# Expert loop with each expert's last product moved between the halves of the next expert's first product, a weight queue in the same order, memory values at every second step, and the first W1 in four column pieces

## The chip, the cores and the metric

The kernel runs on one core of one Trainium2 chip. The metric is the device time of one execution in microseconds (us); the runs of one kernel differ by some tenths of a per cent. TensorE (PE in the profile) multiplies, VectorE (DVE) and ScalarE (ACT) move results out of PSUM and do the element-wise work, GpSimd (POOL) builds selection matrices and issues the indirect transfers, and SyncE (SP) issues the weight transfers.

## What is computed

One layer for 512 prompt tokens and 8 sample tokens, 1024 wide. Three branches (short convolution, stick-breaking attention, attention over a memory of 256 tokens) are gated, summed and multiplied by an output matrix. A mixture of 32 experts follows: each token picks one of four groups and two of its eight experts. Cut to the parts that matter here:

```python
def cross_attend(qx, mk, mv):                       # samples: mk, mv from a cache of 8 requests
    s = jnp.einsum('bthd,bmhd->bhtm', qx, mk) * (X_HEAD_DIM ** -0.5)
    p = jax.nn.softmax(s, axis=-1).astype(mv.dtype)
    return jnp.einsum('bhtm,bmhd->bthd', p, mv)

def run_block(a):                                   # per expert e, on the rows that chose it
    xb, e = a
    return (jax.nn.silu(xb @ w1[e]) * (xb @ w3[e])) @ w2[e]
```

W1 and W3 of an expert are 1024 x 512 and W2 is 512 x 1024, all in float32: 2 MiB each, 6 MiB for an expert, and every expert is run.

## The kernel before, in words

Each engine has its own hand-written program; semaphores order them. Nothing is scheduled by a tool, so the order of the code is the order on each engine and in each queue.

**Front part.** The input projection runs as chunks of 128 columns, each a product in three passes (high times high, high times low, low times high parts; `three_pass`, line 800). In the middle of the kernel eight turns compute a gate chunk (`three_pass`) and a branch chunk (`branch`, line 946) of the convolution branch. Between these products stand sixteen small steps, `point(0)` to `point(15)`, `point(2n)` behind the gate chunk of turn n and `point(2n+1)` behind its branch chunk. The steps carry the attention over the prompt's memory and the sample rows' scores and values. The value products of the eight sample rows are `two_values(0, b, pm_t)` for b = 0, 2, 4, 6, two rows at a time; before, they stand in steps 11, 12, 13 and 14. Their data are the tiles `vals`, two slots of 512 KB. ScalarE issues the transfers (`load_memory_values(b)`, line 1659), and each pair of rows waits for `val_used`, that is until the pair before it has been multiplied. VectorE then adds the halves of the result (`two_out`), and `turn_four` turns them.

**Between the parts.** The output product (`merge_out(i)`, line 1192) runs tile by tile for four prompt tiles, with the router between. It reads `m_hi`, which lies where W1 of expert 0 goes later, so SP waits until all four tiles are done (`wo_ps` at 2 * NT) and then loads W1 of expert 0 in two transfers of 1 MiB. Then come the last 128 rows of `h` into DRAM, W2 of expert 1, W3 and W2 of expert 2.

**Expert loop.** Expert n has slot n % 3 for its weights. PE does for expert n: `up_and_gate` (lines 1379 and 1380: W1 and W3 side by side on the two halves of the array, 16 pairs of matmuls, 8 for each half of the 1024 input rows), `give(n-1, (0, 1))` (line 1401: two of the four tiles of expert n-1's result go back to the tokens by a selection matrix `spread`), `turn_up` and `turn_rows` (transposes, line 767), `give(n-1, (2,))`, `down` (lines 1426 and 1427: W2, 8 pairs), `give(n-1, (3,))`. VectorE copies the up result (`up_out`, line 2556), forms the activation (`act_out`, lines 2563 and 2565), moves the next gathered rows (`rows_out`, line 2545), adds the returned tiles to `x1` (`added`, line 2573) and forms `y_rest` (line 2568) from the down product once ScalarE has written `y_top` (line 1869). Before `y_top`, ScalarE copies the sample rows (line 1865). SP loads for expert e, into the slot of expert e-3: the two halves of W1 and W3 as each half has been used (`up_ps`), then W2 (`y2_ps`). Rows of `h` are gathered by POOL for two experts at a time, 128 rows of 4 KB.

## Time and profile before

| what | value |
|---|---|
| median of 3 runs | 1066.97 us (1065.58 to 1070.71) |
| the profiled execution, its own time | 1069.17 us |
| its span | 1067.3 us |
| PE busy | 1033.1 us, 97% of the span |
| DVE, ACT, POOL busy | 55%, 31%, 14% |
| moved by DMA | 278.42 MB, mean 261 GB/s |
| granted TensorE clock, mean | 0.991 |

Busy is the time in which an engine has an instruction in work. PE's share is high everywhere, so it alone doesn't say whether PE is at its limit: a matmul that waits for weights at its start counts only from its start. The rows of forty slices show PE's share and what the DMA engines moved side by side.

### The profile page before, as it was taken

To read this page: it belongs to the slowest core of one execution; us is meant where nothing else is said; L and a number is where in the kernel's file an instruction comes from. 1 tells how busy PE (TensorE), PEld (TensorE's weight loads), DVE (VectorE), ACT (ScalarE), POOL (GpSimd) and SP (SyncE) were. 2 spreads that over 40 slices of the span, in tenths; PEclk is the share of its full clock that TensorE was granted. 3 is DMA by queue.
4 is the path that set the end of the run, shared out by engine and by line. 5 is a ranking of instruction groups with operands and counts; after the bars stand their busy time and mean duration, and the time that the engine had idled before them with its cause. 6 is when DMAs were issued, how large, how long until landed. Compare 5 with 4: busy or idle time off the path is not lost.

```text
span 1067.3 us, 16248 instructions
## 1 busy us (share of the span) xinstructions
PE 1033.1 (97%) x6634; PEld 696.6 (65%) x6634; DVE 586.4 (55%) x940; ACT 325.6 (31%) x471; POOL 147.2 (14%) x180
## 2 busy tenths in 40 slices
PE   9999999999989999999999999999999999999996
PEld 8999998988868788999776433443334334334432
DVE  5222265877767866543546655555555555455545
ACT  6322233155546544322445011111111111111111
POOL 0000000002313564000000311101111101111100
PEclk9999999999999999999999999999999999999999
DMA  5723131545462232552445999999999999999982
GB/s 203 261 94 98 62 100 60 191 137 182 151 221 75 83 123 87 211 201 83 164 182 220 424 427 424 426 426 427 426 425 425 429 424 426 426 426 429 424 350 80
DMA packets 51274, 278.42 MB, mean 261 GB/s; under 512 B 7542, under 2 KB 7814, under 8 KB 30728
## 3 DMA queue, kind: packets, MB, share of 16 engines
q1 hardware_dynamic: 42360, 254.26, 59.3%
q0 software_dynamic: 6048, 16.86, 4.8%
q10 hardware_dynamic: 2800, 6.36, 1.7%
q8 instruction: 48, 0.79, 0.3%
q14 instruction: 18, 0.15, 0.0%
HBM read 274.09 MB, written 7.48 MB: 264 GB/s over the span
## 4 chain that ended last, share of the span: by engine, by line
PE 86%; DVE 4%; DMA 3%; ACT 2%; POOL 2%; issue 2%; ACTq 0%; SPq 0%; POOLq 0%; DVEq 0%
PE acc_all L800 25%; PE acc_all L1379 20%; PE acc_all L1426 10%; PE acc_all L1401 7%; PE acc_all L767 6%; PE acc_all L946 5%; PE acc_all L1192 3%; POOL beta L435 1%; DMA vals<-in_cache_mem_v 1%; DMA xg<-h_dram,pair_row 1%; PE acc_all L1063 1%; PE acc_all L1427 1%; POOL keep L435 1%; PE acc_all L876 1%; PE acc_all L875 1%
## 5 line engine op out<-in xcount | busy, mean ns | idle before, releaser
L800 PE MATMUL acc_all<-xn_hi,w_hi 128*128 128x260 f32 x832 | 172.3, 289 | 8.7 <-DVE gate_sb L2131 4.3
L800 PE MATMUL acc_all<-xn_hi,w_lo 128*128 128x260 f32 x832 | 168.6, 284 | 0.0
L800 PE MATMUL acc_all<-xn_lo,w_hi 128*128 128x260 f32 x832 | 168.2, 284 | 0.0
L2573 DVE TENSOR_TENSOR x<-x,acc_all 128x1024 f32<-128x1024 f32 x127 | 151.4, 1213 | 1.1 <-PE acc_all L1401 1.1
L800 PEld LDWEIGHTS acc_all<-xn_hi,w_hi 128*128 128x128 f32 x832 | 129.7, 190 | 16.2 <-DVE gate_sb L2131 6.6
L800 PEld LDWEIGHTS acc_all<-xn_lo,w_hi 128*128 128x128 f32 x832 | 129.4, 190 | 0.0
L800 PEld LDWEIGHTS acc_all<-xn_hi,w_lo 128*128 128x128 f32 x832 | 129.2, 190 | 0.0
L724 POOL TENSOR_SCALAR spread<-tok_row,slots 128x512 fp32r<-128x512 f32 x32 | 50.2, 1568 | 370.2 <-PE acc_all L1401 370.2
L1958 DVE TENSOR_TENSOR w_lo<-w_raw,w_hi 128x1024 fp32r<-128x1024 f32 x52 | 63.4, 1222 | 67.7 <-ACT w_hi L1564 67.5
L1865 ACT ACTIVATE few<-acc_all,slots 8x512 f32<-8x512 f32 x64 | 43.4, 679 | 153.5 <-PE acc_all L1427 121.0
L1859 ACT ACTIVATE gate_h<-acc_all 128x256 f32<-128x256 f32 x32 | 12.3, 384 | 234.6 <-PE acc_all L767 234.6
L2556 DVE COPY up_sb<-acc_all 128x512 f32<-128x512 f32 x32 | 22.1, 691 | 104.9 <-PE acc_all L1380 104.9
L1379 PE MATMUL acc_all<-w_a,xg_t 128*64 128x512 f32 x176 | 78.1, 595 | 0.6 <-DVE xg_t L2462 0.6
L1379 PE MATMUL acc_all<-w_b,xg_t 128*64 128x512 f32 x176 | 78.1, 595 | 0.4 <-DVE xg_t L2545 0.4
L1380 PE MATMUL acc_all<-w_b,xg_t 128*64 128x512 f32 x176 | 78.1, 595 | 0.0
L1380 PE MATMUL acc_all<-w_a,xg_t 128*64 128x512 f32 x176 | 78.1, 595 | 0.0
L1379 PE MATMUL acc_all<-w_c,xg_t 128*64 128x512 f32 x160 | 70.8, 595 | 0.1
L1380 PE MATMUL acc_all<-w_c,xg_t 128*64 128x512 f32 x160 | 70.8, 595 | 0.0
L2568 DVE SCALAR_TENSOR_TENSOR y_rest<-acc_all,slots,y_top 128x512 fp32r<-128x512 f32 x32 | 24.0, 750 | 84.8 <-ACT y_top L1869 84.8
L1401 PEld LDWEIGHTS acc_all<-y_top,spread 64*128 64x128 f32 x256 | 23.9, 183 | 58.3 <-issue 32.6
L1401 PE MATMUL acc_all<-y_top,spread 64*128 64x512 f32 x256 | 60.7, 469 | 0.7 <-DVE x L2573 0.7
L1564 ACT ACTIVATE w_hi<-w_raw 128x1024 fp32r<-128x1024 f32 x52 | 54.5, 1051 | 7.4 <-DMA w_raw<-in_w_in 7.4
(389 smaller groups left out, 1855.2 us busy)
## 6 DMA issues: line engine op xcount, KB each, us to landing
w_a<-in_w SPq DMA_DIRECT2D x44, 1024.0 KB, 17.2
w_b<-in_w SPq DMA_DIRECT2D x44, 1024.0 KB, 18.0
w_c<-in_w SPq DMA_DIRECT2D x40, 1024.0 KB, 17.7
w_raw<-in_w_in SPq DMA_DIRECT2D x52, 512.0 KB, 3.7
w_a<-in_w SPq DMA_DIRECT2D x11, 2048.0 KB, 18.3
w_b<-in_w SPq DMA_DIRECT2D x11, 2048.0 KB, 18.6
w_c<-in_w SPq DMA_DIRECT2D x10, 2048.0 KB, 18.7
w_br<-in_w_branch SPq DMA_DIRECT2D x24, 256.0 KB, 4.5
```

Source lines behind the costliest of these rows:

```text
L724: pool.tensor_scalar(spread[n % 2][:, :], tok_row[:, :], slot_tok[:, n:n + 1], None, ALU.is_equal).then_inc(spread_ok, 1)
L767: return pe.transpose(out, in_, ident[0:k, 0:k])
L800: mm = pe.matmul(out[:, a, :], w[:, slot, k, :], x[:, k, a * HALF_TOK:(a + 1) * HALF_TOK], start=first, stop=last)
L946: mm = pe.matmul(out[:, a, :], w, x[:, a * HALF_TOK:(a + 1) * HALF_TOK], start=begin, stop=end)
L1379: pe.matmul(bank(5)[0:CAP, :], lhs, w1_sb[w][:, k, :], start=(k == 0), stop=(k == KD - 1))
L1380: mm = pe.matmul(bank(5)[CAP:P, :], lhs, w3_sb[w][:, k, :], start=(k == 0), stop=(k == KD - 1))
L1401: mm = pe.matmul(bank(out + half), spread[hot][at, tok(t)], y[at, :], start=first and alone, stop=not first, skip_group_check=not alone)
L1426: pe.matmul(bank(7)[0:CAP, :], act_t[:, c, :], w2_sb[w][:, c, 0:DE], start=(c == 0), stop=(c == CW - 1))
L1564: act.activation(w_hi[:, slot, :, :], w_raw[:, slot, :, :], ACT.Copy).then_inc(split_hi, 1)
L1865: act.activation(few[n // QUADS % 2][half][strip:strip + NB, :], bank(7)[at, :], ACT.Copy, scale=slot_gate[at, n:n + 1]).then_inc(few_in, 1)
L1958: dve.tensor_tensor(w_lo[:, slot, :, :], w_raw[:, slot, :, :], w_hi[:, slot, :, :].bitcast(F32), ALU.subtract).then_inc(split_lo, 1)
L2573: dve.tensor_tensor(x1[:, t, :], x1[:, t, :], bank(2 * pair, 2), ALU.add).then_inc(back_ok, 1)
```

## The change

Four edits.

1. **Expert loop on PE.** The product is cut in its halves (`up_part`), and the down product of expert n-1 now stands between the two halves of expert n's up product, with tiles 2 and 3 of expert n-2's result ahead of it. Tiles 0 and 1 of expert n-1 follow the second half. DVE's order follows: two adds come right behind `up_out`, two behind `rows_out`, and `y_rest` of expert n comes last in the turn, now waiting for a down product that PE reaches in the next turn.
2. **Weight queue.** SP loads in the order of use: first half of W1 and W3 of expert e, W2 of expert e-1, second half of W1 and W3 of expert e. Both halves of expert 3 are issued ahead of the loop.
3. **W1 of expert 0** comes in four pieces of 128 columns, each issued when one tile of the output product is done. A piece is 512 KB in runs of 512 bytes.
4. **Memory values.** `two_values(0, b)` stands in steps 11, 13 and 15, and the fourth behind the gate product after the eight turns; `two_out` and `load_memory_values(6)` move with them, and `cross_values(XH - 1)` goes ahead of the two `turn_four`.

```diff
-            sp.wait_ge(wo_ps, 2 * NT)
-            load_up(0, 0, w1_sb, w1_d)
+            for t in range(NT - 1):
+                sp.wait_ge(wo_ps, NT + 2 + t)
+                sp.dma_start(w1_sb[0][:, :, tok(t)], w1_d[0][:, :, tok(t)]).then_inc(w13_ld[0][0], 16)
...
-            def load_expert(e, j, before):
-                load_up(e, j, before=before)
-
+            def load_down(e, j, before):
                 sp.wait_ge(y2_ps, before)
                 sp.dma_start(w2_sb[j][:, :, :], w2_d[e]).then_inc(w2_ld[j], 16)
 
+            def load_turn(e, j, before):
+
+                load_up(e, j, before=before, parts=(0,))
+                load_down(e - 1, (j - 1) % WS, before - 1)
+                load_up(e, j, before=before, parts=(1,))
+
+            load_up(WS, 0, before=1)
             with sp.Fori(0, NE // WS - 1) as i:
-                for j in range(WS):
-                    load_expert(WS * i + WS + j, j, WS * i + j + 1)
...
-                if 11 <= p < 15:
+                if p in (11, 13, 15):
                     pe.wait_ge(pmt_sb, 1)
-                    two_values(0, 2 * (p - 11), pm_t)
+                    two_values(0, p - 11, pm_t)
...
             turn_probs(2 * XH - 1)
+            two_values(0, 6, pm_t)
+            cross_values(XH - 1)
             pe.wait_ge(yg_sb, 4)
             turn_four(0, 0, 5)
             pe.wait_ge(cs_exp, 4 * XH)
             turn_four(0, 1, 6)
-            cross_values(XH - 1)
...
+            for n in range(1, NE):
                 p, j = divmod(n, 2)
-                if n >= 1:
-                    pe.wait_ge(xgt_sb, 2 * p + 2)
-                    pe.wait_ge(up_ok, n)
-                up_and_gate(n % WS, p % 2, j, n // WS + 1, n)
-                if n >= 1:
-                    give(n - 1, (0, 1))
+                w, loads = n % WS, n // WS + 1
+                pe.wait_ge(xgt_sb, 2 * p + 1)
+                pe.wait_ge(up_ok, n)
+                up_part(w, p % 2, j, loads, 0)
...
+                    give(n - 2, (2, 3))
+                    pe.wait_ge(rest_ok, n - 1)
+                    down((n - 1) % WS, (n - 1) // WS + 1, n - 1)
+                pe.wait_ge(xgt_sb, 2 * p + 2)
+                up_part(w, p % 2, j, loads, 1)
+                give(n - 1, (0, 1))
                 pe.wait_ge(up_ok, n + 1)
                 turn_up()
...
+            give(NE - 2, (2,))
+            pe.wait_ge(rest_ok, NE - 1)
+            down((NE - 1) % WS, (NE - 1) // WS + 1, NE - 1)
...
-                if n in (5, 6):
-                    two_out(0, 4 * (n - 5))
+                if n >= 5:
+                    two_out(0, 2 * (n - 5))
```

How the instructions move. In the rows below, `w_a`, `w_b`, `w_c` are the three weight slots, "waits" names the semaphores, and "..." stands for the rest of a run of matmuls.

PE, one turn in the middle of the expert loop (up product in slot a), before:

```order
L1379 MATMUL acc_all<-w_a,xg_t 64x512 [waits w13_ld0a,up_ok,xgt_sb]
...
L1379 MATMUL acc_all<-w_a,xg_t 64x512 [waits w13_ld0b]
...
L1401 MATMUL acc_all<-y_top,spread_180 128x512 [waits rest_ok,spread_ok,back_ok]
...
L767 MATMUL acc_all<-ident,up_sb 128x128 [waits up_ok]
...
L767 MATMUL acc_all<-ident,xg_173 128x128 [waits xgt_sb,xg_ld1]
...
L1401 MATMUL acc_all<-y_top,spread_180 128x512 [waits back_ok]
...
L1426 MATMUL acc_all<-w_a,act_t 64x512 [waits actt_ok,w2_ld0,rest_ok]
...
L1401 MATMUL acc_all<-y_top,spread_180 128x512 [waits back_ok]
...
```

The same turn in the changed kernel:

```order
L1385 MATMUL acc_all<-w_a,xg_t 64x512 [waits w13_ld0a,up_ok,xgt_sb]
...
L1400 MATMUL acc_all<-y_top,spread_179 128x512 [waits back_ok]
...
L1425 MATMUL acc_all<-w_c,act_t 64x512 [waits actt_ok,w2_ld2,rest_ok]
...
L1385 MATMUL acc_all<-w_a,xg_t 64x512 [waits w13_ld0b,xgt_sb]
...
L1400 MATMUL acc_all<-y_top,spread_180 128x512 [waits rest_ok,spread_ok,back_ok]
...
L775 MATMUL acc_all<-ident,up_sb 128x128 [waits up_ok]
...
L775 MATMUL acc_all<-ident,xg_172 128x128 [waits xgt_sb,xg_ld0]
...
```

The down product (slot c, the expert before) now stands between the two halves of the up product; the transposes `up_sb` are no longer followed by the product that needs their activation.

DVE, the same turn, from the activation to the copy of the next up result, before:

```order
L2565 TENSOR_TENSOR act_t<-gate_h,acc_all 128x128 [waits half_ok]
L2545 TENSOR_TENSOR xg_t<-acc_all,norm_pk 128x512 [waits xgt_ps]
L2573 TENSOR_TENSOR x_103<-x_103,acc_all 128x1024 [waits back_ps] x2
L2568 SCALAR_TENSOR_TENSOR y_rest<-acc_all,slots,y_top 128x512 [waits top_ok]
L2573 TENSOR_TENSOR x_103<-x_103,acc_all 128x1024 [waits back_ps]
L2556 COPY up_sb<-acc_all 128x512 [waits upt_ps,up_ps]
L2573 TENSOR_TENSOR x_103<-x_103,acc_all 128x1024 [waits back_ps]
```

and in the changed kernel:

```order
L2576 TENSOR_TENSOR act_t<-gate_h,acc_all 128x128 [waits half_ok]
L2556 TENSOR_TENSOR xg_t<-acc_all,norm_pk 128x512 [waits xgt_ps]
L2584 TENSOR_TENSOR x_103<-x_103,acc_all 128x1024 [waits back_ps] x2
L2579 SCALAR_TENSOR_TENSOR y_rest<-acc_all,slots,y_top 128x512 [waits top_ok]
L2567 COPY up_sb<-acc_all 128x512 [waits upt_ps,up_ps]
L2584 TENSOR_TENSOR x_103<-x_103,acc_all 128x1024 [waits back_ps] x2
```

The adds (`x_103` is `x1`) now come in two pairs, and nothing stands between `y_rest` and the copy of the up result.

## Rows read from the trace of the kernel before

**Rows 1.** The page: PE's busy time, and DMA share in 40 slices.

```profile
PE 1033.1 (97%) x6634; PEld 696.6 (65%) x6634; DVE 586.4 (55%) x940; ACT 325.6 (31%) x471; POOL 147.2 (14%) x180
...
DMA  5723131545462232552445999999999999999982
```

**Rows 2.** Stretches of the span: busy time by engine, PEclk, DMA share, GB/s.

```profile
core 0: us, PE busy (x) PEld busy (x) DVE busy (x) ACT busy (x) POOL busy (x), PEclk, DMA share, GB/s
300.00:304.50 4.50, 3.27 (x15) 1.64 (x16) 3.98 (x6) 1.20 (x4) 1.89 (x2) 0.62 0.24 62
555.00:565.00 10.00, 10.00 (x59) 8.71 (x59) 5.80 (x26) 6.01 (x7) 0.00 (x0) 1.00 0.14 54
740.00:840.00 100.00, 99.23 (x508) 39.51 (x506) 51.98 (x76) 17.00 (x28) 15.25 (x11) 1.00 1.01 427
```

**Rows 3.** DVE's copies of the up result, one an expert, all 32.

```profile
L2556 DVE COPY up_sb<-acc_all x32: 690/692/694, 594.7 to 1046.6; 128x512 f32<-128x512 f32 x32
```

**Rows 4.** Timeline from expert 30 to 31: start, duration, engine, instruction [idle before].

```profile
1032.12 0.50 PE L1401 MATMUL acc_all<-y_top,spread 64*128 64x512 f32 x2
1035.22 0.61 PE L1426 MATMUL acc_all<-w_a,act_t 128*64 128x512 f32 x1 [0.31 <-DVE act_t L2565]
1038.91 1.38 ACT L1865 ACTIVATE few<-acc_all,slots 8x512 f32<-8x512 f32 x2 [4.48 <-PE acc_all L1427]
1039.47 0.64 PE L1379 MATMUL acc_all<-w_b,xg_t 128*64 128x512 f32 x1
1041.04 0.75 DVE L2568 SCALAR_TENSOR_TENSOR y_rest<-acc_all,slots,y_top 128x512 fp32r<-128x512 f32 x1 [3.19 <-ACT y_top L1869]
1042.95 0.59 PE L1379 MATMUL acc_all<-w_b,xg_t 128*64 128x512 f32 x1
1046.49 0.50 PE L1401 MATMUL acc_all<-y_top,spread 64*128 64x512 f32 x2
1049.58 0.61 PE L1426 MATMUL acc_all<-w_b,act_t 128*64 128x512 f32 x1 [0.31 <-DVE act_t L2565]
```

**Rows 5.** SP's queue: the last loads of expert 31, second half and W2.

```profile
1004.40 3.01 SPq L546 DMA_DIRECT2D w_b<-in_w  x1
1010.18 0.33 SPq L580 DMA_DIRECT2D w_b<-in_w  x1
```

**Rows 6.** Time to landing: W3 half at 1004.40, W2 at 1010.18, W2 at 603.25.

```profile
DMA to landing us min/median/max: 30.4/30.4/30.4
DMA to landing us min/median/max: 29.5/29.5/29.5
DMA to landing us min/median/max: 12.3/12.3/12.3
```

**Rows 7.** SP's queue ahead of the expert loop.

```profile
572.08 1.06 SPq L546 DMA_DIRECT2D w_a<-in_w  x2
577.65 0.33 SPq L569 DMA_DIRECT2D h_dram<-h_tok  x1
578.02 0.43 SPq L570 DMA_DIRECT2D w_b<-in_w  x1
584.24 1.39 SPq L546 DMA_DIRECT2D w_c<-in_w  x2
```

**Rows 8.** Chain of waits, steps 11 to 13.

```profile
292.09 9.00 DMA vals<-in_cache_mem_v
```

**Rows 9.** PE's timeline, steps 12 to 15.

```profile
301.23 1.94 PE L997 MATMUL acc_all<-vals,pm_t 128*32 128x512 f32 x8 [1.77 <-DMA vals<-in_cache_mem_v]
303.10 0.80 PE L946 MATMUL acc_all<-y_hi_conv,w_br_hi_conv 128*128 128x260 f32 x2
306.72 0.49 PE L956 MATMUL acc_all<-q_parts,both_r 40*128 40x512 f32 x1
310.07 1.06 PE L997 MATMUL acc_all<-vals,pm_t 128*32 128x512 f32 x8 [0.95 <-DMA vals<-in_cache_mem_v]
319.95 0.51 PE L946 MATMUL acc_all<-y_hi_conv,w_br_hi_conv 128*128 128x260 f32 x2
323.01 0.50 PE L956 MATMUL acc_all<-q_parts,both_r 40*128 40x512 f32 x1
```

**Rows 10.** A gate chunk in the chain, and DMA issues of 512 KB: time to landing.

```profile
492.71 5.74 PE acc_all L800 x48
...
w_raw<-in_w_in SPq DMA_DIRECT2D x52, 512.0 KB, 3.7
vals<-in_cache_mem_v ACTq DMA_DIRECT2D x8, 512.0 KB, 5.1
```

More of the change, by code:

```diff
@@ L536, in _, with load_up @@
                 load_branch(n + RING)
-            def load_up(e, j, *which, before=None):
-                for part in range(2):
+            def load_up(e, j, *which, before=None, parts=range(2)):
+                for part in parts:
                     if before is not None:
@@ L1369, in turn_rows, with up_part @@
                 turn_pair(p % 2, half)
[L1371 to L1388 removed]
+            def up_part(w, slot, j, loads, part):
+                pe.wait_ge(w13_ld[w][part], 32 * loads + (FIRST_LOADS[part] if w == 0 else 0))
+                for k in range(part * KD // 2, (part + 1) * KD // 2):
+                    lhs = xg_t[:, slot, k, CAP * j:CAP * (j + 1)]
+                    pe.matmul(bank(5)[0:CAP, :], lhs, w1_sb[w][:, k, :], start=(k == 0), stop=(k == KD - 1))
+                    mm = pe.matmul(bank(5)[CAP:P, :], lhs, w3_sb[w][:, k, :], start=(k == 0), stop=(k == KD - 1))
+                mm.then_inc(up_ps, 1)
             def turn_up():
@@ L1690, in _ @@
                     load_memory_values(max(0, 2 * (n - 4)))
-                if n == 6:
-                    load_memory_values(6)
                 if n % 2 == 0 and n >= 2:
@@ L2597, in _ @@
                 if n >= 1:
-                    added(n - 1, (0,))
+                    added(n - 1, (0, 1))
                 else:
                     over_first()
+                if n == 1:
+                    rows_out(1, 0)
                 dve.wait_ge(sig_ok, n + 1)
@@ L2617, in _ @@
                 elif n == 1:
-                    rows_out(1, 0)
+                    rows_out(1, 1)
                 elif n + 2 < NE:
@@ L2621, in _ @@
                 if n >= 1:
-                    added(n - 1, (1, 2) if n < NE - 1 else (1, 2, 3))
-                if n == 1:
-                    rows_out(1, 1)
-                dve.wait_ge(top_ok, n + 1)
-                y_rest_out(slot_gate[:, n:n + 1])
-                if 1 <= n < NE - 1:
-                    added(n - 1, (3,))
+                    added(n - 1, (2, 3))
+                if n >= BATCH and n % BATCH == 0:
+                    add_few(n // BATCH - 1)
                 if n == 1:
```

72 lines of the change are left out of this document (32 added, 40 removed).

## Prediction

> **What bounds the kernel now.** Four views, in this order. The page first: PE is busy 97% of the span, and from the 23rd slice on DMA is full as well [rows 1]; two resources may bind in the second half. The stretches tell what "full" is: 427 GB/s at a share of 1.01 [rows 2]. An expert needs 6.29 MB of weights and half of a gather (0.26 MB), 6.55 MB, so the transfers take 15.3 us an expert. PE takes less: from the give of expert 30's turn at 1032.12 to that of expert 31 at 1046.49 is 14.37 us [rows 4], and over all 31 steps (1046.6 - 594.7) / 31 = 14.6 us with the start and the long turns [rows 3]. So PE sets the pace and eats a store of loads that were issued early. The queue's view shows it: a W2 load took 12.3 us to land at the start of the loop and the last ones took 30 us [rows 6], though each is issued as soon as its slot is free. The last view is how much store is left at the end: the second half of W3 of expert 31 lands at 1004.40 + 30.4 = 1034.8, W2 at 1010.18 + 29.5 = 1039.7 [rows 5, 6]; PE needs them at 1042.95 and 1049.58 [rows 4]. That is 8.15 and 9.9 us. **A faster PE can win those 8.15 us and no more, unless the stream itself ends earlier.** Ahead of the loop PE is alone, so what it saves there moves PE and the stream together.
>
> **Memory values.** Step 12 waits 1.77 us for its transfer (9.00 us long) and step 13 waits 0.95 us [rows 8, 9]. Behind the first wait the granted clock in 300 to 304.5 is 0.62 of full speed [rows 2], between the levels of 1.2 and 2.4 GHz: step 12's values take 1.87 us to the next product instead of about 1.0, and the branch chunk 306.72 - 303.10 = 3.62 instead of 323.01 - 319.95 = 3.06 [rows 9]. Together 1.77 + 0.87 + 0.56 + 0.95 = 4.2 us. In the new order a gate chunk (5.74 us, [rows 10]), a branch chunk (3.06) and the small products lie between two value steps, over 10 us, against 9.00 us for the longest load: no wait. The fourth pair has only the gate chunk and a transpose ahead of it, about 6.3 us, against 5.1 us at the median [rows 10] and 9.00 at the worst: between no wait and 3 us. ScalarE's `load_memory_values(6)` also holds its next split back until step 15, which the gate chunk covers. I take -4.2, bounds -4.4 and -1.
>
> **First W1.** In 555 to 565 the queues move 54 GB/s [rows 2]; three of the four pieces (1.57 MB) now go there, at no cost to anybody. But the stream isn't shortened by all of 1.57 / 0.427 = 3.7 us: SP issues the fourth piece at 572.08, then must wait for `h` at 577.65 and for the router at 584.24 [rows 7], so the queue now runs dry at two places. By 584.24 SP had issued 4.7 MB before (W1, `h`, W2); 12.2 us at 427 would carry 5.2 MB, less some 2 us of start (an estimate), 4.3. So 0.4 MB stood over, and up to 1.1 if the stream was slower in its start; now next to nothing to 0.6. The stream behind it gains 1 to 2 us; I take 1.6. What no row shows is a hardware-queue load in runs of 512 bytes. From below, a piece costs its bytes, 1.2 us. From above, each run costs as much as a 4 KB one, eight times the bytes, 9.8 us: then the last piece takes 4.9 us more than the whole W1 did, and the stream loses 4.9 instead of gaining 1.6. I take the bytes, since `w_raw`, of the same 512 KB, lands in 3.7 us [rows 10], start included, and the last piece isn't needed for 14 us. The Trainium skill, "DMA: Bandwidth & Descriptors", section "Measured (HBM→SBUF, 128 partitions, SWDGE, issued from GpSimd)", speaks against cutting: it asks for 1 MiB or more a transfer, gives 341 GB/s there and 138 GB/s at 64 KB. By it, an estimate, a piece takes 1.5 to 3.8 us instead of 1.2, and my gain of 1.6 would be -1.0 to 1.3. No run here shows it yet.
>
> **Expert loop, PE.** Work is the same: 16 and 8 pairs, four tiles given back, eight transposes. What goes is the wait of the down product for the activation, 0.31 us [rows 4], since half an up product and two tiles now stand between; and of six changes between kinds of product one goes (up, give, turn, give, down, give before; up, give, down, up, give, turn now). A change shows as the rest between 8 pairs at 0.43 us (3.44) and the 3.54 us from 1042.95 to 1046.49 [rows 4]: 0.1. I take 0.41 us a turn, bounds 0.15 (a part given back by the cut in the up product) and 0.6. For experts 3 to 31 that is 29 x 0.41 = 11.9 us. In the turns of experts 1 and 2 two things cancel: the wait for both halves of the turned rows goes, but two adds now stand ahead of `rows_out`; I take +0.6 for them, bounds -1 and +2.
>
> A wait is added: tiles 0 and 1 of expert n-1 need `y_rest`, whose down product now ends only half an up product earlier. Its chain, from ACT's start at 1038.91 to DVE's end at 1041.04 + 0.75 = 1041.79, is 2.9 us, 3.1 with the start [rows 4]; the cover is the half, 3.5 us. It is hidden with 0.4 us to spare. Behind `y_rest` on DVE stands the copy of the up result, which needs the same half to end, so it isn't held up.
>
> **Weight queue.** The new order is PE's new order. With the stream's end at 1039.7 - 4.2 - 1.6 = 1033.9, and 4.9 us for 2.1 MB, W2 of expert 31 lands at 1033.9, the second half of W1 and W3 at 1029.0, W2 of expert 30 at 1024.1, the first half at 1019.2. A PE that nobody holds reaches the second half at 1042.95 - 4.2 + 0.6 - 11.9 = 1027.5, so it waits 1.5 us there. In the old order the first half would land 4.9 us later, when PE has long asked for it: this edit gives nothing by itself and is what lets the first be used.
>
> **Sum.** PE alone: -4.2 + 0.6 - 11.9 = -15.5 us. The stream: -4.2 - 1.6 - 8.15 = -13.95. The smaller holds, and both ends lie so close that I take -13.9. The profiled execution, 1069.17 us, is 2.2 us above the median; against it 1055.3, against the median 1066.97 **1053.1 us**, -1.3%. A measurement of this kernel tells 0.5%, 5.3 us, from no change.
>
> **Rivals.**
> - *The turn gains little* (0.15 us: the cut costs what the wait gave). PE: -4.2 + 0.6 - 4.4 = -8.0, 1059.0. For it: PE's rests between kinds of product are modelled, not measured. Chance 0.15.
> - *A front edit fails*: pieces at the upper bound, -13.95 + 6.5 = -7.4, 1059.5; or a full wait for the fourth pair, -11, 1056. Chance 0.13.
> - *The clock falls in the loop.* At the end PE waits for weights in each turn. After 1.77 us of waiting the clock was halved at 301, which cost 1.4 us; the wait of 0.95 us at 309 brought nothing [rows 2, 9]. One to three such drops: -12.5 to -9.7, 1054.5 to 1057.3. Chance 0.10. The Trainium skill, "TensorE: Matmul & The Clock Gate", section "HAM oscillation — how this bites in real kernels", has this as a pattern of loops that wait for loads; by the rows above it needs longer waits than I forecast.
> - *The loop closes over `y_rest`* (slower). The give waits whenever ACT's copy of the sample rows, `y_top` and `y_rest` take more than 3.5 us. Each us over is paid 29 times. It eats all of -15.5 when the chain is 4.03 us, and at 4.4 us the kernel is at 1066.97 - 15.5 + 26 = 1077.5. Against it: the rows give 3.1 us, and no new work on either engine. Chance 0.04.
> - *The interleaving does nothing* because some other wait holds each turn at 14.37: only the front gain, 1062.8. Chance 0.05.
> - *The stream ends earlier than I think* (all 3.7 us of the pieces): 1051.5, or 1050. Chance 0.05.
>
> **The numbers.** The forecast has 0.48, with 1051.5 to 1055.5 as its own range. The range 1049.5 to 1060.5 leaves out the slower case, the no-gain case and the edges of the others. Faster by over 0.5% are all but the last part of the front failures, the `y_rest` case and the no-gain case: 0.89; within 0.5%: 0.07; slower 0.04.
>
> **What would show it.** No wait for `vals` in steps 11 to 15, and no low clock near 300. The last W2 lands about 5.8 us earlier than at 1039.7. Turns of about 13.95 us in the middle of the loop, near 15.3 at the very end with PE waiting for weights, and the down product without the 0.31 us for `act_t`. Wrong would be: a wait of the give for `y_rest` in every turn; turns of 14.3; DMA that isn't full between 600 and 1030.

## The result, and the profile after

The changed kernel takes 1059.03 us (median of 6 runs, 1057.1 to 1063.23) against 1067.88 us for the kernel before on the same chip: a ratio of 0.9938, 95% interval 0.9917 to 0.9959. Timed again later beside its variants it came to 1058.72 us and a ratio of 0.9908 (0.9889 to 0.9928). So the change gives 0.6 to 0.9%, 7 to 10 us, where 1.3% was forecast. One of the twelve executions of experiment 1 below took 3538.6 us; it counts as slow and is left out of the ratio. The profiled execution has a span of 1060.5 us and took 1062.32 us; forecast for it was 1055.3 us, 7.0 less.

The page of the changed kernel: PE's busy time, the DMA share in 40 slices, and the chain that ended last.

```profile
PE 1024.3 (97%) x6634; PEld 692.2 (65%) x6634; DVE 586.5 (55%) x940; ACT 325.6 (31%) x471; POOL 147.0 (14%) x180
...
DMA  5632232545453242452454999999999999999993
...
PE 76%; DMA 9%; SPq 5%; DVE 4%; ACT 2%; POOL 2%; issue 2%; ACTq 0%; POOLq 0%; DVEq 0%
```

The chain now holds 9% of DMA and 5% of SP's queue, against 3% and 0% before: the weights are on it. DVE's copies of the up result, one an expert, cut the run into three parts:

```profile
L2567 DVE COPY up_sb<-acc_all x32: 690/692/694, 594.6 to 1039.5; 128x512 f32<-128x512 f32 x32
```

Against [rows 3]: up to the first copy 594.7 became 594.6, where -4.2 was forecast; from the first copy to the last 451.9 became 444.9, -7.0 where -9.75 (8.15 of store and 1.6 of a shorter stream) was; from the last copy to the end 20.7 became 21.0. What is missing is 4.1 + 2.7 + 0.3 = 7.1 us. So two terms failed, one ahead of the loop, one in the stream. The two executions are alike ahead of the loop: both have four low clocks there, three at the same places (near 120, 219 and 577 us) and one in the memory values (near 301 before, 328 now).

**The turn takes the forecast time.** Two copies in a row, and the new cover of `y_rest` (start, duration, engine, instruction, idle time before):

```profile
641.10 0.69 DVE L2567 COPY up_sb<-acc_all 128x512 f32<-128x512 f32 x1 [0.56 <-PE acc_all L1386]
655.07 0.69 DVE L2567 COPY up_sb<-acc_all 128x512 f32<-128x512 f32 x1 [0.56 <-PE acc_all L1386]
...
665.62 1.38 ACT L1877 ACTIVATE few<-acc_all,slots 8x512 f32<-8x512 f32 x2 [8.36 <-PE acc_all L1426]
667.02 0.69 ACT L1881 ACTIVATE y_top<-acc_all,slots 128x512 fp32r<-128x512 f32 x1
667.74 0.75 DVE L2579 SCALAR_TENSOR_TENSOR y_rest<-acc_all,slots,y_top 128x512 fp32r<-128x512 f32 x1 [3.83 <-ACT y_top L1881]
668.93 0.50 PE L1400 MATMUL acc_all<-y_top,spread 64*128 64x512 f32 x2
```

A turn takes 13.97 to 13.99 us, against 14.36 before; every eighth, which has the sample rows' product as well, takes 14.95 (15.34 before). `y_rest` is done at 668.49 and the give starts at 668.93: 0.44 us to spare.

The time isn't made up as forecast, though. The 0.31 us wait of the down product in [rows 4] stands only in the last two turns, which have no `turn_rows`. In the middle of the loop the kernel before looks like this:

```profile
788.34 0.50 PE L1401 MATMUL acc_all<-y_top,spread 64*128 64x512 f32 x2
...
788.75 0.29 DVE L2565 TENSOR_TENSOR act_t<-gate_h,acc_all 128x128 f32<-128x128 f32 x1
...
789.18 0.61 PE L1426 MATMUL acc_all<-w_b,act_t 128*64 128x512 f32 x1
```

No wait is shown before the down product. It does start 0.14 us behind the end of its activation (789.04; 0.15 us in the last turns), and 0.84 us behind the start of the tile ahead of it, where the same kind of product ahead of an up product takes 0.66: 0.18 us that can be called waiting. One turn of each kernel by its parts, each from its first product to the next part's, in us:

| | up | tiles given back | transposes | down | turn |
|---|---|---|---|---|---|
| before (786.09 to 800.45) | 7.02 | 1.14 + 0.84 + 0.66 | 1.11 | 3.59 | 14.36 |
| change (643.22 to 657.20) | 3.58 + 3.54 | 1.13 + 1.14 | 1.11 | 3.48 | 13.98 |

So 0.18 us are the wait for the activation, 0.19 come from giving tiles 2 and 3 back together (1.32 became 1.13), 0.11 from a shorter down product (why isn't shown), and the cut in the up product takes 0.10 back.

**The memory values** still have a wait. PE's timeline, and the chain around it:

```profile
326.59 1.07 PE L1005 MATMUL acc_all<-vals,pm_t 128*32 128x512 f32 x8 [1.86 <-DMA vals<-in_cache_mem_v]
327.59 3.59 PE L993 MATMUL acc_all<-prob_t,mv 128*128 128x512 f32 x4
...
332.07 2.43 PE L1071 MATMUL acc_all<-proj 64*128 64x256 f32 x16
```

```profile
316.94 1.49 ACT y_hi_x L1730
318.43 0.33 ACTq L1672
...
318.79 7.66 DMA vals<-in_cache_mem_v
```

Both waits of [rows 9] are gone. The fourth pair waits 1.86 us, and behind that wait the clock goes down, as it did behind step 12's in [rows 2]:

```profile
core 0: us, PE busy (x) PEld busy (x) DVE busy (x) ACT busy (x) POOL busy (x), PEclk, DMA share, GB/s
300.00:304.50 4.50, 4.50 (x28) 3.45 (x27) 4.43 (x6) 1.62 (x5) 1.89 (x2) 1.00 0.14 32
326.00:331.00 5.00, 4.41 (x13) 1.44 (x14) 1.38 (x2) 0.00 (x0) 0.00 (x0) 0.68 0.00 0
555.00:565.00 10.00, 10.00 (x60) 8.67 (x60) 5.80 (x26) 6.00 (x7) 0.00 (x0) 1.00 0.47 150
575.00:580.00 5.00, 4.94 (x20) 2.17 (x22) 4.22 (x19) 3.54 (x4) 0.00 (x0) 0.70 0.47 145
606.00:608.00 2.00, 2.00 (x46) 1.58 (x46) 0.39 (x3) 0.36 (x1) 1.24 (x2) 1.00 0.83 279
740.00:840.00 100.00, 100.00 (x522) 39.85 (x521) 56.27 (x81) 16.98 (x28) 15.21 (x11) 1.00 1.01 426
```

The first two rows are that low clock: gone from 300, back at 327. The other four are the stream. 555 to 565 now moves 150 GB/s (54 before), but 575 to 580 has a share of 0.47, and 606 to 608 one of 0.83. (PEclk of 0.70 in 575 to 580 is a low clock that the kernel before has at the same place.) The same two stretches before:

```profile
575.00:580.00 5.00, 4.87 (x20) 2.08 (x22) 4.21 (x19) 3.61 (x4) 0.00 (x0) 0.74 0.99 409
606.00:608.00 2.00, 2.00 (x29) 0.88 (x26) 0.00 (x0) 0.00 (x0) 1.78 (x3) 1.00 1.01 430
```

SP's queue in the changed kernel, with the issues around both:

```profile
544.34 28.20 SPq L569 DMA_DIRECT2D w_a<-in_w  x4
577.58 0.34 SPq L571 DMA_DIRECT2D h_dram<-h_tok  x1
...
584.12 1.32 SPq L547 DMA_DIRECT2D w_c<-in_w  x2
...
589.60 5.92 SPq L547 DMA_DIRECT2D w_a<-in_w  x4
606.30 0.82 SPq L547 DMA_DIRECT2D w_b<-in_w  x2
607.38 0.33 SPq L580 DMA_DIRECT2D w_a<-in_w  x1
```

Between 572.5 and 577.58 SP waits for `h`; between 595.5 and 606.30 it waits for a buffer, and the first half of expert 4 and W2 of expert 3 come only then (W2 of expert 3 at 603.25 before, [rows 6]). At the end of the loop the stream is late. SP's last loads, the time to landing of the two halves at 1001.70 to 1006 and of the last W2, and PE's waits:

```profile
1001.70 4.29 SPq L547 DMA_DIRECT2D w_b<-in_w  x2
1006.03 2.41 SPq L580 DMA_DIRECT2D w_b<-in_w  x1
```

```profile
DMA to landing us min/median/max: 29.0/30.4/31.8
DMA to landing us min/median/max: 34.4/34.4/34.4
```

```profile
1020.73 0.61 PE L1385 MATMUL acc_all<-w_a,xg_t 128*64 128x512 f32 x1 [0.43 <-DMA w_a<-in_w]
1035.78 0.62 PE L1385 MATMUL acc_all<-w_b,xg_t 128*64 128x512 f32 x1 [1.29 <-DMA w_b<-in_w]
```

W3's second half lands at about 1003.87 + 31.8 = 1035.7 and PE takes it at 1035.78; before, it landed at 1034.8 and was used at 1042.95. The last W2 lands at 1040.4 (1039.7 before, 1033.9 forecast). The last four turns take 14.46, 15.88, 14.62 and 15.05 us. **The stream ends as late as before, and now PE waits for it.** Between 1000 and 1030 the DMA share is 1.00 to 1.02, so it is the bytes that are late.

### The profile page after: what moved, and what is told of

Same layout as the page of the kernel before. It is cut to its first block, busy times and chain, and to the rows that moved or that the text cites. A ratio compares the mean times of both kernels' runs of the same rounds, so it can differ in the third digit from the quotient of the medians.

```text
span 1060.5 us, 16298 instructions
## 1 busy us (share of the span) xinstructions
PE 1024.3 (97%) x6634; PEld 692.2 (65%) x6634; DVE 586.5 (55%) x940; ACT 325.6 (31%) x471; POOL 147.0 (14%) x180
## 4 chain that ended last, share of the span: by engine, by line
PE 76%; DMA 9%; SPq 5%; DVE 4%; ACT 2%; POOL 2%; issue 2%; ACTq 0%; POOLq 0%; DVEq 0%
PE acc_all L808 26%; PE acc_all L1385 15%; PE acc_all L1425 8%; DMA w_b<-in_w 6%; PE acc_all L954 6%; PE acc_all L1400 5%; PE acc_all L775 5%; SPq L547 4%; PE acc_all L1201 3%; DMA xg<-h_dram,pair_row 1%; POOL beta L436 1%; PE acc_all L1071 1%; SPq L580 1%; PE acc_all L993 1%; PE acc_all L974 1%
## 5 line engine op out<-in xcount | busy, mean ns | idle before, releaser
L1385 PE MATMUL acc_all<-w_b,xg_t 128*64 128x512 f32 x176 | 79.7, 596 | 1.6 <-DMA w_b<-in_w 1.6
L1385 PE MATMUL acc_all<-w_a,xg_t 128*64 128x512 f32 x176 | 79.7, 596 | 1.0 <-DVE xg_t L2473 0.6
L1386 PE MATMUL acc_all<-w_b,xg_t 128*64 128x512 f32 x176 | 79.8, 596 | 0.0
L1386 PE MATMUL acc_all<-w_a,xg_t 128*64 128x512 f32 x176 | 79.8, 596 | 0.0
L1385 PE MATMUL acc_all<-w_c,xg_t 128*64 128x512 f32 x160 | 72.5, 595 | 2.6 <-DVE xg_t L2556 1.5
L1386 PE MATMUL acc_all<-w_c,xg_t 128*64 128x512 f32 x160 | 72.5, 596 | 0.0
L1400 PE MATMUL acc_all<-y_top,spread 64*128 64x512 f32 x256 | 57.5, 444 | 0.6 <-DVE x L2584 0.6
L1585 ACT ACTIVATE proj<-acc_all 128x520 f32<-128x520 f32 (+1 forms) x28 | 16.9, 604 | 124.8 <-PE acc_all L808 118.8
L1385 PEld LDWEIGHTS acc_all<-w_b,xg_t 128*64 128x64 f32 x176 | 23.0, 137 | 47.4 <-issue 47.2
```

The source lines that it names most:

```text
L1385: pe.matmul(bank(5)[0:CAP, :], lhs, w1_sb[w][:, k, :], start=(k == 0), stop=(k == KD - 1))
L1386: mm = pe.matmul(bank(5)[CAP:P, :], lhs, w3_sb[w][:, k, :], start=(k == 0), stop=(k == KD - 1))
L1400: mm = pe.matmul(bank(out + half), spread[hot][at, tok(t)], y[at, :], start=first and alone, stop=not first, skip_group_check=not alone)
```

## The experiments

Two yardsticks stand in each profile, and they are steadier than the absolute times, since low clocks in the front part come and go between executions (the first copy of an up result lay between 587.7 and 596.7 us). *Stretch V* runs from the values of step 11 to the first scores. *Loop L* runs from the first copy of an up result to the last. L has a spread of its own: five profiles whose loop and weight queue are those of the change (the change twice, experiments 2, 6 and 14) lie between 444.5 and 445.6 us. Turns of 13.98 us below always mean those that aren't every eighth.

**1. The values alone**: before, with the value steps of the change.

```diff
-                if 11 <= p < 15:
-                    two_values(0, 2 * (p - 11), pm_t)
+                if p in (11, 13, 15):
+                    two_values(0, p - 11, pm_t)
...
+            two_values(0, 6, pm_t)
+            cross_values(XH - 1)
             pe.wait_ge(yg_sb, 4)
...
-            cross_values(XH - 1)
```

`load_memory_values(6)` and `two_out` move with them as in the change.

> The kernel before with only the value steps moved (the fourth edit). Theory A (the fourth pair's transfer is now the wait): PE waits about 1.9 us for vals behind the gate product, the clock may drop there, and the first score product starts 0 to 1 us earlier than at 332.6; the whole is 0 to 1 us faster than before. Rival (my forecast's term): no wait, -4.2 us, 1063.7. A third outcome, the wait moves but the clock doesn't fall in most runs: about -2 us.

1065.91 us, ratio 0.9993 (0.9979 to 1.0006): nothing that the times can tell. The fourth pair waits 1.76 us; V is 39.31 us. Theory A holds, the forecast's term doesn't.

**2. All but the values**: the change, with the edit of experiment 1 undone.

> The changed kernel with the value steps as before; the other three edits stay. Theory A and the theory that the stream of weights sets the end: the same as the changed kernel within 1 us, since both begin the stream at nearly the same time (1059 to 1060). If the value steps did carry something in ordinary runs, this one is up to 2 us slower than the changed kernel.

1062.09 us, ratio 0.9956 (0.9942 to 0.997). Two waits, 1.51 and 1.33 us, a low clock at 301.4, V 42.35. With the clock the same on both sides the edit shows its worth in V:

| | old value steps | new value steps |
|---|---|---|
| low clock in V | 42.08 (before), 42.35, 42.97 (experiment 8) | 41.12 (change), 41.07 |
| none | 40.41 (experiment 3) | 39.2 to 39.5 (ten profiles) |

1.0 to 1.9 us, not 4.2. By the times this run is 3.1 to 3.4 us above the change (1059.03 and 1058.72), more than the expectation's 2 us and more than V shows, while experiment 1 was only 0.8 us below the kernel before. The clock is what differs: the mean granted clock is 0.993 in these twelve executions, 0.994 in those of the change and 0.9955 in those of experiment 6. With 1060 us times the share of clock that was withheld taken off each execution, an estimate, the edit is worth 1.6 us in experiment 1 (against the kernel before) and 1.5 us here (against experiment 6, timed beside it), which is what V says.

The low clock lies in V in three of the four profiles with the old steps and in two of the twelve with the new. Whether the new steps make it rarer isn't settled by so few; over whole executions experiment 1's mean clock (0.993) is no higher than that of the kernel before (0.994).

**3. The loop alone**: before, with PE's interleaved order, and the old queue, W1 and values.

```diff
-            for n in range(NE):
+            up_part(0, 0, 0, 1, 0)
...
+            for n in range(1, NE):
```

> The kernel before with only the interleaved expert loop: the queue in the old order, W1 of expert 0 in two transfers, value steps as before. Stream theory: turns of 13.98 us until the store of loads is used up, then PE waits for first halves that stand in the queue behind W2s and second halves; the end is 3 to 6 us before that of the kernel before, 1062 to 1065. Rival (the order of the queue doesn't matter, since it is full and bytes decide): within 1 us of the changed kernel, 1059 to 1060.

1065.03 us, ratio 0.998 (0.9966 to 0.9995). Turns of 13.98 us to the copy of expert 22, then 14.38, 15.41, 15.62 (an eighth turn), 14.41, 14.71, 17.6: PE waits for the half that the old order issues late, and behind one wait the clock is down in the loop. L is 448.6 us. The stream theory holds, the rival falls. PE's timeline and the stretch behind it:

```profile
983.75 1.09 PE L1377 MATMUL acc_all<-w_b,xg_t 128*64 128x512 f32 x1 [1.90 <-DMA w_b<-in_w]
```

```profile
983.50:987.50 4.00, 3.75 (x10) 1.27 (x12) 0.80 (x2) 0.00 (x0) 0.00 (x0) 0.57 1.02 432
```

**4. The old queue order**: the change, with `load_expert` as before.

```diff
-                load_up(e, j, before=before, parts=(0,))
-                load_down(e - 1, (j - 1) % WS, before - 1)
-                load_up(e, j, before=before, parts=(1,))
+                load_up(e, j, before=before)
+                sp.wait_ge(y2_ps, before)
+                sp.dma_start(w2_sb[j][:, :, :], w2_d[e]).then_inc(w2_ld[j], 16)
```

> The changed kernel with SP's loop in the old order (both halves of W1 and W3 of an expert, then its W2). Stream theory: no dry spot at 606 to 608, so the stream ends some 0.5 us earlier, but the first half of expert 31 and W2 of expert 30 change places: PE waits for the second half when it has it all; the end within 1.5 us of the changed kernel, rather slower. Rival (the order is what makes the loop work, as I wrote in the prediction): 3 to 5 us slower.

1064.36 us, ratio 0.9965 (0.9947 to 0.9982), L 448.9. The same late turns and the same low clock (984.7). The order is worth 3 to 6 us to the changed kernel; without it L gains 3.0 us instead of 7.0, the low clock's price included. Here the rival holds, and my theory (within 1.5 us) falls.

**5. W1 whole**: the change, with W1 of expert 0 in two transfers of 1 MiB.

```diff
-            for t in range(NT - 1):
-                sp.wait_ge(wo_ps, NT + 2 + t)
-                sp.dma_start(w1_sb[0][:, :, tok(t)], w1_d[0][:, :, tok(t)]).then_inc(w13_ld[0][0], 16)
+            sp.wait_ge(wo_ps, 2 * NT)
+            load_up(0, 0, w1_sb, w1_d)
```

> The changed kernel with W1 of expert 0 in two transfers of 1 MiB at 572. Stream theory: at 192 MB to go the stream is about 0.5 us later than in the changed kernel, but the dry spot at 606 to 608 shrinks, so the end is the same within 1 us. Rival (my forecast's term): 1.6 us slower or more.

1058.81 us, ratio 0.9927 (0.9899 to 0.9954), L 444.8 against 444.9: the pieces give nothing here.

**6. The last values issued early**, on ScalarE.

```diff
+            load_memory_values(6)
             act.wait_ge(br_ps, KD)
             act.wait_ge(cy_sb, XH - 1)
             act.activation(y_hi_x[:, 0:XH - 1, 0:SEQ], proj[:, B0:B0 + XH - 1, 0:SEQ], ACT.Copy).then_inc(xt_hi, 1)
-            load_memory_values(6)
```

> The changed kernel, but ScalarE issues the last memory values before its 1.49 us copy of y_hi_x instead of behind it. Theory A: the transfer starts about 1.1 us earlier, PE's wait falls from 1.86 to 0.5 to 0.9 us, and the clock doesn't fall there; the scores start 2.5 to 3.5 us earlier and the whole is as much faster than the changed kernel (1056). Rival: the transfer is slow because it meets the weight chunk's load, so it lands when it did; no gain.

1058.26 us, ratio 0.9915 (0.9897 to 0.9934). The wait stays, 1.99 us, and V is 39.54. The load goes out as soon as step 15's values have freed the buffer, and takes its 7.8 us. In the changed kernel ScalarE's copy (316.94 to 318.43) lay beside those same values (done at 318.29), so it held the load up by 0.14 us at most. Theory A falls; there is no gain, as the rival says, but for another reason than the rival's. The chain of this version:

```profile
313.71 1.04 PE acc_all L1005 x8
...
314.78 0.37 ACTq L1672
...
315.18 7.79 DMA vals<-in_cache_mem_v
```

**7. Half of W2, changed kernel.**

```diff
-                sp.dma_start(w2_sb[j][:, :, :], w2_d[e]).then_inc(w2_ld[j], 16)
+                sp.dma_start(w2_sb[j][:, 0:CW // 2, :], w2_d[e][:, 0:CW // 2, :]).then_inc(w2_ld[j], 16)
```

> The changed kernel, but from expert 3 on W2's load brings only half of W2 (the first two of four row groups of each partition), so the stream is 17% lighter; the products still run on the whole tile and their results are not the reference's. Stream theory: PE never waits for weights, turns of 13.98 us to the end, the end 4.1 us earlier than in the changed kernel's profile, that is 1055 in the median. Rival (PE waits for something else at the end): the end stays.

1056.18 us, ratio 0.9885 (0.9849 to 0.9922). No wait for weights at all, turns of 13.98 us to the end (the last is 13.54), L 440.2: the stream theory holds. This is PE alone: 451.9 - 440.2 = 11.7 us saved, where the forecast had 11.9 - 0.6 = 11.3. The stream withholds 4.7 of them.

**8. Half of W2, kernel before**, by the same edit.

> The kernel before, whose W2 loads bring only half of each matrix from expert 3 on (so that the stream is 1.05 MB an expert shorter; the output leaves out computing with the right half of W2). My theory: the kernel before is set by PE in the whole loop, its weights were 8 us early at the end, so a lighter stream gives nothing: ratio 0.997 to 1.003, turns of 14.36 us as before, last periods 14.36. Rival (the stream held the kernel before as well, by contention of its transfers with the gathers or by something the waits don't show): 3 to 5 us faster, as with the same cut in the changed kernel, which gave 0.4% against the changed kernel.

1068.61 us, ratio 1.0008 (0.999 to 1.0027), L 451.7. Before, the stream set nothing; the theory holds. The copies of the two, this one and experiment 7:

```profile
L2556 DVE COPY up_sb<-acc_all x32: 691/692/694, 595.4 to 1047.1; 128x512 f32<-128x512 f32 x32
```

```profile
L2567 DVE COPY up_sb<-acc_all x32: 691/692/694, 592.9 to 1033.1; 128x512 f32<-128x512 f32 x32
```

**9. The stream started early**: the change, with W2 of expert 1 right behind W1's last piece, W2 of expert 2 right behind `h` (ahead of the wait for the router), and W2 of expert 3 as soon as expert 0 has used its buffer.

```diff
+            sp.dma_start(w2_sb[1][:, :, :], w2_d[1]).then_inc(w2_ld[1], 16)
             sp.wait_ge(h_ok, NT)
             sp.dma_start(h_dram[tok(MERGE_TILES[NT - 1]), :], h_tok[:, MERGE_TILES[NT - 1], :]).then_inc(h_st, 16)
-            sp.dma_start(w2_sb[1][:, :, :], w2_d[1]).then_inc(w2_ld[1], 16)
+            sp.dma_start(w2_sb[2][:, :, :], w2_d[2]).then_inc(w2_ld[2], 16)
...
-            sp.dma_start(w2_sb[2][:, :, :], w2_d[2]).then_inc(w2_ld[2], 16)
...
             load_up(WS, 0, before=1)
+            load_down(WS, 0, 1)
```

The first three turns of SP's loop are written out, so that the W2 of expert 3 isn't loaded twice.

> The changed kernel with the stream filled in at its start: W2 of experts 1 and 2 are issued right behind the last piece of W1 (W2 of expert 2 behind the rows of h), and W2 of expert 3 as soon as expert 0's is used. Stream theory: the stream ends 4 to 6 us earlier, PE hardly waits any more, the end is 3.5 to 4.5 us earlier than the changed kernel's, 1055. Rival (the waits at the end come from SP's full queue or from the order, not from bytes): no gain. Another rival: the last rows of h land later behind W2 and the first gather with them, which costs 1 to 3 us at the start.

1057.05 us, ratio 0.9892 (0.9854 to 0.993), L 442.3: 2.6 us of the 4.7. The stream theory has the direction, but forecast more: the stream ends 2.6 us earlier, not 4 to 6, and the last two turns are still long (14.56 and 15.09).

**10. Only W2 of expert 3 early**: the last line of 9's diff alone, with the first turns written out as there.

> The changed kernel with one load moved: W2 of expert 3 is issued as soon as expert 0 has used its buffer, not behind the first half of expert 4, where the new order of the queue puts it. My theory: the dry spot at 606 to 608 us goes (DMA share there from 0.83 to 1.0), the stream ends about 1 us earlier measured from the start of the loop, and since the stream sets the end the kernel is 0.5 to 1.2 us faster than the changed one: ratio 0.9925 to 0.993 against before. Rival 1 (what the queue lost there it makes good later, or the gain of the run with both loads moved came from the two loads ahead of the loop): no change against the changed kernel, 0.9938. Rival 2: that run's 2 us all came from this load: 0.991 to 0.992.

1058.21 us, ratio 0.9922 (0.9896 to 0.9948), L 445.2. The dry spot is gone (share 1.03 in 606 to 608), the loop isn't shorter: the first rival.

**11. Only W2 of experts 1 and 2 ahead**: 9's diff without its last line.

> The changed kernel with W2 of experts 1 and 2 issued right behind the last piece of W1 and behind h, ahead of the wait for the router, and W2 of expert 3 where the change has it. My theory: the column pieces moved 1.6 MB into an idle stretch, but the queue then ran dry at the wait for h (share 0.47 in 575 to 580 us, before 0.99), so that nothing came of it; with W2 behind them the stream ends 1.5 to 2.6 us earlier measured from the first copy of an up result (445.5 us in the changed kernel, 442.9 with both moves, 445.9 with the move of W2 of expert 3 alone): 443 to 444, and the last copy 442.3 to 443.4 us behind the first. Rival (both moves are needed): 444.5 or more.

1059.2 us, ratio 0.9921 (0.9901 to 0.9941), L 444.4. My theory wanted 442.3 to 443.4; the rival, that both moves are needed, has it (it said 444.5 or more). The stretches show why:

```profile
596.00:598.00 2.00, 2.00 (x12) 0.76 (x10) 1.82 (x7) 0.00 (x0) 0.00 (x0) 1.00 1.04 438
598.00:600.00 2.00, 2.00 (x12) 0.60 (x10) 1.84 (x5) 0.00 (x0) 0.00 (x0) 1.00 0.66 279
600.00:602.00 2.00, 2.00 (x18) 0.62 (x14) 0.00 (x0) 0.00 (x0) 1.92 (x4) 1.00 0.00 0
602.00:604.00 2.00, 2.00 (x46) 1.39 (x44) 0.52 (x3) 0.60 (x1) 1.07 (x1) 1.00 0.49 78
```

The stream came 4 us early to the point at which SP waits for the next free buffer, and stood still there for as long.

**12. W1 whole, and W2 ahead**: the diffs of 5 and 9.

> The changed kernel with W1 of expert 0 whole, as two transfers of 1 MiB behind the last of its space, W2 of experts 1 and 2 right behind it (ahead of the waits for h and for the router), and W2 of expert 3 as soon as its buffer is free. My theory: the column pieces are worth nothing once the queue has W2 to go on with, since it is full behind W1 in either case, or the later start of W1 costs up to 1.5 us because the pieces used an idle stretch: ratio 0.989 to 0.9915, against 0.9892 with the pieces. Rival (pieces of 512-byte runs cost queue time that the whole transfers don't): faster than with the pieces by 1 us or more, 0.988 or less.

1058.18 us, ratio 0.9919 (0.9893 to 0.9945), L 444.1. My theory is not borne out as it stood: without the pieces L is 1.8 us longer than with them (442.3; 442.7 and 441.5 in experiments 15 and 16), while the times don't part the two. The pieces are worth something once the queue has W2 to go on with, about the 1.6 us that the prediction gave them; only one profile stands on the side without pieces.

**13. The changed kernel again**, as a level for the last set.

> The changed kernel itself, unchanged, beside the variants of this set. It is the level against which they are read: so far variants that should have gained little (0.9922, 0.9919, 0.9915, 0.9927) all came out below the changed kernel's own 0.9938. If that figure was a high sample, it comes out at 0.991 to 0.993 here; if the variants gain, it stays at 0.9935 to 0.994. In the profile: a wait of 1.7 to 2.0 us for the values of the fourth pair, turns of 13.98 us, and 444.5 to 445.5 us from the first copy of an up result to the last.

1058.72 us, ratio 0.9908, L 445.6, V 39.24: its two ratios, 0.9938 and 0.9908, have overlapping intervals, so that 0.9938 needn't be the better figure, and none of experiments 5, 6, 10, 11 and 12 differs from the change by its time. Their verdicts rest on the stretches of their profiles. Nor do the intervals of 9 and 15 part them from the change; there L does (442.3 and 442.7, outside 444.5 to 445.6).

**14. Cross values first**, on PE.

```diff
-            two_values(0, 6, pm_t)
             cross_values(XH - 1)
+            two_values(0, 6, pm_t)
```

> The changed kernel with the product of the last head's cross values put ahead of the fourth pair's values, so that 2 us of PE work lie over the wait. My theory: the memory values' edit brought 1.0 us and not 4.2 because the wait for the fourth pair (1.76 to 1.99 us) took the place of the two waits removed, so hiding part of it shortens the stretch from the values of step 11 to the first scores from 39.35 us (all profiles without a low clock in it) to 38.0 to 38.6 us, with a wait of 0 to 0.7 us for ScalarE's copy in its place; the whole kernel by up to 1 us, which the times can't tell. Rival (the wait isn't on the path: PE would only wait at the scores or the next gate chunk, as it waits 0.86 us for VectorE behind them now): the stretch gets shorter, but a later wait grows by the same, and the next gate chunk starts 14.2 us after the fourth pair's landing as before.

1060.68 us, ratio 0.9932 (0.9913 to 0.9951). The wait for the values is gone, and V is **longer**, 40.12 us. PE's timeline, and two pieces of the chain:

```profile
325.61 1.98 PE L993 MATMUL acc_all<-prob_t,mv 128*128 128x512 f32 x4 [0.74 <-ACT prob_t L1662]
327.53 1.07 PE L1005 MATMUL acc_all<-vals,pm_t 128*32 128x512 f32 x8
330.19 1.09 PE L775 MATMUL acc_all<-ident,y_four 128*128 128x128 f32 x8 [1.60 <-DVE y_four L2173]
331.22 2.43 PE L1071 MATMUL acc_all<-proj 64*128 64x256 f32 x16
```

```profile
324.47 0.60 ACT gate_sb L1652
325.07 0.50 ACT prob_t L1662
```

My theory falls here, and the rival too, since V isn't shorter at all: behind the fourth pair stand VectorE's two steps that make `y_four` (0.69 and 0.70 us), and the cross values had covered them. Moved away, they leave a wait of 1.60 us, and ScalarE's copy one of 0.74. In the change this place is held by a chain: step 15 ends, transfer of 7.7 us, values, `y_four`, turn. In this order another takes over, which has no transfer in it: gate product, ScalarE's two copies, cross values, values, `y_four`, turn. The order of the change is the better one by V (0.8 us); the times don't tell.

**15 and 16. Both repairs**, 6 and 9 together; then with 14 as well.

> The changed kernel with both repairs: ScalarE issues the last memory values ahead of its copy, and the queue has W2 of experts 1 and 2 right behind the last piece of W1 and W2 of expert 3 as soon as its buffer is free. My theory: the two are in different stretches and add, 0.2% of the first (0.9915 against 0.9938) and 0.46% of the second (0.9892): ratio 0.986 to 0.989, 1053 to 1057 us, waits for weights only in the last two or three experts. Rival (the first was only a run without the low clock in the front part, so it gives nothing): 0.989 to 0.990, like the second alone, with the wait for the fourth pair's values at 1.5 to 2 us either way.

1055.56 us, ratio 0.9901 (0.9875 to 0.9928), L 442.7; turns longer than 13.98 us only at the end (14.33 and 15.71). The wait for the fourth pair stays at 1.82 us, V at 39.38: the two don't add, only the stream's repair shows, as the rival says.

> All repairs together: ScalarE issues the last memory values ahead of its copy, the last cross values ahead of them on PE, W2 of experts 1 and 2 right behind W1's last piece and W2 of expert 3 as soon as its buffer is free. My theory: they add, 0.5 to 1.1 us below the version without the change on PE (0.9901, 1055.56 us): ratio 0.988 to 0.990. Rival (front gains come and go with the low clock, and only the stream counts): 0.990 to 0.991.

1056.94 us, ratio 0.9897 (0.9875 to 0.9919), L 441.5, V 40.12. The version of 15 is the fastest by its median, 11 us below the kernel before and 3 us below the change; the intervals of 9, 15 and 16 don't part them. The ratio of 16 lies in its forecast range all the same, by luck: what was to bring it, V, is longer as in 14.

**Where the stream's lead goes.** The table gives when so many MB were still to come up to the last weight packet (bytes of the trace's packets summed from there backwards, without those that fetch instructions), in us from the first copy of an up result:

| | 192 MB | 184 MB | 182 MB | end | L |
|---|---|---|---|---|---|
| before | -10.3 | 8.9 | 13.7 | 444.6 | 451.9 |
| change | -11.1 | 8.3 | 13.8 | 445.5 | 444.9 |
| change again (13) | -9.9 | 9.6 | 14.4 | 446.2 | 445.6 |
| W1 whole (5) | -10.5 | 8.6 | 14.1 | 445.5 | 444.8 |
| W2 of 3 early (10) | -11.2 | 8.3 | 13.1 | 445.9 | 445.2 |
| W2 of 1, 2 ahead (11) | -15.1 | 4.6 | 13.5 | 445.1 | 444.4 |
| W1 whole, all W2 early (12) | -10.4 | 9.0 | 13.9 | 444.8 | 444.1 |
| pieces, all W2 early (9) | -13.6 | 5.7 | 10.6 | 442.9 | 442.3 |

From 184 to 182 MB the full rate takes 4.7 us; experiment 11 takes 8.9. Pieces alone gain nothing. Without pieces, all three W2 early (12) end 0.7 us before the change, no more than the change's two profiles differ. Pieces and W2 of 1 and 2 have a lead of 4 us that is lost at the next buffer; only with W2 of expert 3 to put there does a lead last, 3.2 us at 182 MB and 2.6 at the end.

The table also shows what the 2.7 us are that the stream fell short: it was to end 1.6 us earlier from the first copy on than before, and it ends 0.9 us later (1.6 in the second profile). About 0.8 us of that are lost behind 182 MB in both profiles of the change (0 to 1.9 us in the variants); no experiment says where.

## Why the prediction was wrong where it was

- **Expert loop, PE: the size right, its terms not.** 13.98 us a turn for 13.95; PE alone 11.7 us for 11.3; no wait for `y_rest`, 0.44 us to spare for 0.4. But the 0.31 us for the activation were read in the last two turns and multiplied by 29; in the middle of the loop they are 0.18 at most. And no change between kinds of product goes: both orders in the prediction's brackets have six. What goes instead is one of the three groups of tiles, 0.19 us. That 0.41 lies so near the measured 0.38 is luck.
- **What bounds it: right.** "A faster PE can win those 8.15 us and no more, unless the stream itself ends earlier." It won 7.0, or 6.3 when profiled again, with a stream that ended 0.9 and 1.6 us later; experiment 7 shows PE free to win 11.7, and experiment 8 that the stream set nothing before.
- **Weight queue: right** that the old order would hold PE; the price, which the prediction didn't give, is 3 to 6 us (experiment 4). That the new order gives nothing by itself wasn't run.
- **Memory values: the step that failed.** The sum was 1.77 + 0.87 + 0.56 + 0.95. Two parts of it weren't the edit's. The fourth pair was given "between no wait and 3 us" and then priced at none; it waits 1.6 to 2.0 us in all twelve profiles that have it in this place, and the rows had hinted at it: 6.3 us of cover against loads of 5.1 to 9.0 us, of which the pair's second counts (7.7 in the change). And 0.87 + 0.56 = 1.43 us was the low clock of one execution, which comes and goes with either order. 4.2 less both, 1.8 and 1.43, leaves 1.0, the lower end of what V shows (1.0 to 1.9). In the two profiled executions even that doesn't reach the first copy: the parts ahead of V and behind it are 0.45 and 0.4 us longer, which is within what they vary by.
- **First W1: failed as well.** 1.6 us were forecast (1 to 2), nothing came (experiment 5). The prediction saw that the queue now runs dry at two places and counted only up to the second, 584. It didn't follow the lead further, to the point at which SP waits for a buffer that PE frees. There a lead lasts only if a load is left that may go. The new queue order made that worse: it puts W2 of expert 3 behind a half that isn't free yet (L 444.4 in experiment 11, 442.3 in experiment 9).
- The price of a run of 512 bytes was taken right, near the bytes: the three pieces that go alone land in 4.0 to 4.2 us (the first, behind other loads, in 10.7), next to 3.6 for `w_raw` of the same size, and no run shows the queue slower for them. The Trainium skill, "DMA: Bandwidth & Descriptors", section "Measured (HBM→SBUF, 128 partitions, SWDGE, issued from GpSimd)", asks for 1 MiB and more a transfer. Experiments 9 and 12 show that here 512 KB pieces lose nothing, and that L is 1.8 us shorter with them where the queue behind them is fed.
- **The clock in the loop**: a rival that the change itself escaped and experiments 3 and 4 met, a turn of 17.6 us for one of about 15. Behind a wait of 1.90 us the granted clock is 0.57 in 983.5 to 987.5, between the levels of 1.2 and 2.4 GHz. The Trainium skill, "TensorE: Matmul & The Clock Gate", section "HAM oscillation — how this bites in real kernels", describes loops that fall to the low clock because they wait for loads. The row at 983.50 agrees for that one wait; unlike the page's case, the other late turns of the same execution kept the clock.

Of the rivals "a front edit fails" came true, but it priced the pieces and the fourth pair's wait as alternatives, 1059.5 or 1056. That 1059.0 was measured, next to the first, is luck: the pieces never cost eight times their bytes. Both edits fell short at once, one by 2.3 to 3.2 us and the other by 1.6, for reasons that have nothing to do with each other, and that case had no line.

## What to carry to other kernels

Read a price in the turns to which it will be applied: the first and last turns of a loop leave work out, and a wait there can be absent in the middle. A lead of a load stream is worth only what the next free buffer lets through: follow it issue by issue to the place where the queue waits for the consumer, and see whether a load is left to go there. When waits in a row of steps are spread over more work, price the last step of the row by its own cover, and look at what hangs behind it, before calling the waits gone. And take a low clock seen in one execution out of an edit's price, until a second profile has it too.

## What the runs showed of the hardware that was not expected

- A wait of the same length brings a low clock in some executions only. The fourth pair waits 1.6 to 2.0 us in twelve profiles, and the granted clock falls to the level of 1.2 GHz behind it in two of them. Such a stretch costs about 1.7 us (V 41.1 against 39.35).
- With about 30 us of transfers outstanding, SP's own issues take long: 4.29 us for two at 1001.70 and 2.41 for one at 1006.03, against 0.82 for two at 606.30. The outstanding time alone doesn't decide it: in the kernel before, with 30 us to landing as well, one issue took 3.01 us and another 0.33 [rows 5].
- Loads in runs of 512 bytes, 512 KB each, land in 4.0 to 4.2 us on the hardware queue when nothing stands ahead of them.
